# Cross-attention values as three products of rounded high and low parts, in a two-block transformer kernel

## The reference

```python
def memory_cross_attention(h, m, wq, wkv, wo):
    q = (h @ wq).reshape(B, S, XA_HEADS, XA_HEAD_DIM)      # 4 heads of 256
    kv = m @ wkv                                           # m: 256 normalised memory tokens
    k = kv[..., :D].reshape(B, -1, XA_HEADS, XA_HEAD_DIM)
    v = kv[..., D:].reshape(B, -1, XA_HEADS, XA_HEAD_DIM)
    s = jnp.einsum('bshd,bmhd->bhsm', q, k).astype(jnp.float32) * (XA_HEAD_DIM ** -0.5)
    p = jax.nn.softmax(s, axis=-1).astype(v.dtype)
    o = jnp.einsum('bhsm,bmhd->bshd', p, v).reshape(B, S, D)
    return o @ wo
```

## Time and profile before

| what | value |
|---|---|
| median of 3 runs | 986.03 us |
| the profiled execution, device time | 985.85 us |
| its span, first to last instruction | 984.0 us |
| PE busy (matmul) | 970.5 us, 99% |
| PE weight loads busy | 879.6 us, 89% |
| DVE busy | 685.7 us, 70% |
| ACT busy | 556.0 us, 57% |
| POOL busy | 207.1 us, 21% |
| granted TensorE clock, mean | 0.998 of 2.4 GHz |
| DMA | 172.94 MB, 176 GB/s |

### The profile page before, as it was taken

How to read it: one execution, slowest core, us unless ns; L and a number is a source line. 1 busy time by engine, 2 the same in 40 slices (tenths; PEclk the granted TensorE clock), 3 DMA queues, 4 the chain that set the end, 5 groups by cost and what they waited for, 6 DMA issues and landing times.

```text
span 984.0 us, 16670 instructions
## 1 busy us (share of the span) xinstructions
PE 970.5 (99%) x6532; PEld 879.6 (89%) x6532; DVE 685.7 (70%) x1057; ACT 556.0 (57%) x857; POOL 207.1 (21%) x197
## 2 busy tenths in 40 slices
PE   9999999999999999999999999999999999999997
PEld 7779769989988988898899899998898989989985
DVE  5789776854666587575566779776687666767973
ACT  5556674675765474555455466555445555546662
POOL 0002033300344540021003015121044301202610
PEclk9999999999999999999999999999999999999999
DMA  9644517465334447355414654467546433555431
GB/s 363 241 135 169 174 42 264 164 214 215 129 129 144 173 134 270 110 188 197 172 53 168 211 211 171 171 213 279 175 168 256 171 129 109 191 181 187 169 149 43
DMA packets 24832, 172.94 MB, mean 176 GB/s; under 512 B 2752, under 2 KB 2880, under 8 KB 4416
## 3 DMA queue, kind: packets, MB, share of 16 engines
q1 hardware_dynamic: 23040, 160.66, 46.0%
q10 hardware_dynamic: 1728, 11.40, 3.1%
HBM read 166.81 MB, written 5.24 MB: 175 GB/s over the span
## 4 chain that ended last, share of the span: by engine, by line
PE 95%; DVE 1%; ACT 1%; DMA 1%; POOL 1%; issue 0%; SPq 0%; ACTq 0%; DVEq 0%
PE banks L537 37%; PE banks L628 16%; PE banks L543 14%; PE banks L545 7%; PE banks L535 6%; PE banks L690 4%; PE banks L744 2%; DMA raw<-w 1%; PE banks L795 1%; PE banks L796 1%; PE banks L777 1%; PE banks L760 1%; PE banks L958 1%; PE banks L875 0%; PE banks L975 0%; PE banks L492 0%
## 5 line engine op out<-in xcount | busy, mean ns | idle before, releaser
L1648 DVE TENSOR_TENSOR wl<-raw,wh 128x1024 fp32r<-128x1024 f32 x300 | 379.0, 1273 | 151.5 <-ACT wh L1132 150.0
L1132 ACT ACTIVATE wh<-raw 128x1024 fp32r<-128x1024 f32 x300 | 313.4, 1054 | 175.6 <-PE banks L537 69.0
L543 PE MATMUL banks<-xx,wh 128*128 128x512 f32 x544 | 192.5, 398 | 0.0
L537 PE MATMUL banks<-xx,wh 128*128 128x256 f32 x1024 | 190.3, 285 | 0.0
L537 PE MATMUL banks<-yy,wh 128*128 128x256 f32 x1000 | 183.5, 285 | 0.1
L537 PEld LDWEIGHTS banks<-xx,wh 128*128 128x128 f32 x1024 | 161.5, 192 | 1.4 <-issue 0.5
L537 PEld LDWEIGHTS banks<-yy,wh 128*128 128x128 f32 x1000 | 156.9, 192 | 1.4 <-issue 0.8
L545 PE MATMUL banks<-xx,wl 128*128 128x256 f32 x544 | 151.9, 279 | 0.0
L537 PE MATMUL banks<-xx,wl 128*128 128x256 f32 x512 | 145.0, 283 | 0.0
L537 PE MATMUL banks<-yy,wl 128*128 128x256 f32 x500 | 136.8, 283 | 0.0
L543 PEld LDWEIGHTS banks<-xx,wh 128*128 128x128 f32 x544 | 102.1, 188 | 22.7
(11 more groups left out here) (227 smaller groups left out, 1462.3 us busy)
## 6 DMA issues: line engine op xcount, KB each, us to landing
raw<-w SPq DMA_DIRECT2D x149, 1024.0 KB, 4.8
m_scratch<-yy ACTq DMA_DIRECT2D x2, 1024.0 KB, 5.2
k_scratch<-kt ACTq DMA_DIRECT2D x2, 1024.0 KB, 7.0
kt<-k_scratch ACTq DMA_DIRECT2D x2, 1024.0 KB, 5.8
yy<-m_scratch ACTq DMA_DIRECT2D x2, 1024.0 KB, 6.8
raw<-w SPq DMA_DIRECT2D x2, 512.0 KB, 5.3
h<-xt SPq DMA_DIRECT2D x2, 512.0 KB, 6.1
v<-memt ACTq DMA_DIRECT2D x1, 1024.0 KB, 7.8
```

The source lines that it names most:

```text
L537: return pe.matmul(b[:, j, :], weights, o_[:, kk, :], start=k0 + k == 0 and q == 0 and (j == 0 or not both_open), stop=k0 + k == KT * p.de ...
L543: pe.matmul(b[:, j, :], wh[:, slot, j, k * P:k * P + P], operand[:, :, tile0 + k0 + k, :], start=k0 + k == 0, stop=False, skip_group_check ...
L1132: act.activation(wh[:, n % 2, j, :], raw[:, n % RAW_SLOTS, j, :], ACT.Copy).then_inc(hi_ready, 1)
L1648: dve.tensor_tensor(wl[:, n % 2, j, :], raw[:, n % RAW_SLOTS, j, :], wh[:, n % 2, j, :].bitcast(F32), ALU.subtract).then_inc(lo_ready, 1)
```

## The change

In X0 and X1 the values and the transposed probabilities are kept as fp32r high and low parts. PE multiplies high probabilities with high and with low values, and then low probabilities with high values. ACT's two evacuations now write the rounded part (`v_r`, and the first of `turned_parts`), and DVE gets two new kinds of instruction: `values_low` (4 per layer, in the value projection) and `turned_low` (4 per layer, in the attention). Both read the PSUM bank that ACT has just copied. The new tensors are other views of memory that is already there (`vl_r` lies in the upper half of `qz`). Two semaphores, `mv_low` and `p_low`, are new.

```diff
@@ project and project_tokens, PE
+                if p.name == "qx1":
+                    pe.wait_ge(mv_low, 8)
...
                                 pe.wait_ge(evac[p.prev.reader], p.prev.end)
+                                if name == "qx0":
+                                    pe.wait_ge(mv_low, 4)
...
                             if c >= 2 and c % 2 == 0 and half == 0:
                                 pe.wait_ge(evac[p.reader], p.base + c - 1 + t)
+                                if name[0:2] == "vx":
+                                    pe.wait_ge(mv_low, 4 * int(name[2]) + 1 + t)
@@ turn_probs, PE
                     pe.wait_ge(t_evac, u - 1)
+                    if name[0] == "X":
+                        pe.wait_ge(p_low, 4 * int(name[1]) + a - 1)
@@ values, PE
-                    for o, sl in value_ops(a):
-                        pe.matmul(o, v[:, 0, sl], wk(4 + a % 2)[:, 0:S], start=True, stop=False)
-                        mm = pe.matmul(o, v[:, 1, sl], wk(4 + a % 2)[:, S:2 * S], start=False, stop=True)
+                    if name[0] == "X":
+                        i = int(name[1])
+                        if a == 0:
+                            pe.wait_ge(mv_low, 4 * i + 4)
+                        for low in range(2):
+                            if low:
+                                pe.wait_ge(p_low, 4 * i + a + 1)
+                            pr = turned_parts(a)[low]
+                            for j, (o, sl) in enumerate(value_ops(a)):
+                                for q in range(2):
+                                    for part in (v_r, vl_r)[0:1 if low else 2]:
+                                        mm = pe.matmul(o, part[:, q, sl], pr[:, S * q:S * q + S],
...
@@ memory_values, ACT
-                act.activation(v[:, t, columns(c)], b, ACT.Copy, scale=rt_m[:, t:t + 1]).then_inc(act_evac, 1)
+                act.activation(v_r[:, t, columns(c)], b, ACT.Copy, scale=rt_m[:, t:t + 1]).then_inc(act_evac, 1)
@@ DVE
+            def values_low(l):
+                p = PH["vx" + l]
+                def f(c):
+                    if c % 2:
+                        for t in range(2):
+                            at = slice(CW * (c - 1), CW * (c + 1))
+                            dve.wait_ge(act_evac, p.base + c + t)
+                            dve.scalar_tensor_tensor(vl_r[:, t, at], bank[p.pair + t][:, :], rt_m[:, t:t + 1],
+                                                     v_r[:, t, at].bitcast(F32), ALU.mult, ALU.subtract).then_inc(mv_low, 1)
+            def turned_low(name, a):
+                if a >= 2:
+                    dve.wait_ge(o_full, OBASE[name] + a - 1)
+                dve.wait_ge(t_evac, UBASE[name] + a + 1)
+                high, low = turned_parts(a)
+                dve.tensor_tensor(low, bank[6 + a % 2][:, :], high.bitcast(F32), ALU.subtract).then_inc(p_low, 1)
@@ plain_low, DVE
                 def f(t):
+                    if name[0] == "X" and 2 <= t < 6:
+                        turned_low(name, t - 2)
...
-                    chunks("vx1", split=3)
+                    chunks("vx1", split=3, between=values_low("1"))
...
-                    chunks("vx0")
+                    chunks("vx0", between=values_low("0"))
```

More of the change, by code:

```diff
@@ L218, in build, with rounded_view @@
         yh, yl = [yy[:, q, :, :] for q in range(2)]
+        def rounded_view(name, shape):
+            with nc.sbuf_tensor(name, shape, F32R) as r:
+                return r
+        qz_r = rounded_view("qz_r", [P, NH, S])
         qz = sb("qz", [P, NH, S])
         kt = sb("kt", [P, KT, S])
+        v_r = rounded_view("v_r", [P, 2, D])
         v = sb("v", [P, 2, D])
         gt = sb("gt", [P, KT, S])
+        work_r = rounded_view("work_r", [P, 12 * 512])
         work = sb("work", [P, 12 * 512])
@@ L340, in turned, with turned_parts @@
             return wk(4 + a % 2)
+        vl_r = qz_r[:, 8:16, :].rearrange("p a b -> p (a b)").rearrange("p (t n) -> p t n", t=2)
+        def turned_parts(a):
+            return [work_r[:, 512 * i:512 * i + 512] for i in (4 + a % 2, 7 + a % 2)]
         def turned_kept(name):
@@ L405, in build @@
         m_hi, m_lo = sem("m_hi"), sem("m_lo")
+        mv_low, p_low = sem("mv_low"), sem("p_low")
         bias_ready, zero_ready, padded = sem("bias_ready"), sem("zero_ready"), sem("padded")
@@ L793, in values @@
                         pe.wait_ge(dve_evac, PH["fourier" if name == "N" else "q" + name.lower()].end)
-                    for o, sl in value_ops(a):
-                        pe.matmul(o, v[:, 0, sl], wk(4 + a % 2)[:, 0:S], start=True, stop=False)
-                        mm = pe.matmul(o, v[:, 1, sl], wk(4 + a % 2)[:, S:2 * S], start=False, stop=True)
+                    if name[0] == "X":
[10 more added lines that the diff above has]
+                                        mm = pe.matmul(o, part[:, q, sl], pr[:, S * q:S * q + S],
+                                                       start=j == q == low == 0 and part is v_r, stop=low == q == 1,
+                                                       skip_group_check=True)
+                    else:
+                        for o, sl in value_ops(a):
+                            pe.matmul(o, v[:, 0, sl], wk(4 + a % 2)[:, 0:S], start=True, stop=False)
+                            mm = pe.matmul(o, v[:, 1, sl], wk(4 + a % 2)[:, S:2 * S], start=False, stop=True)
                     mm.then_inc(o_full, 1)
@@ L1238, in turned_out @@
                 n = 3 * P if name == "A" else 4 * P
-                act.activation(turned(name, a)[:, 0:n], bank[6 + a % 2][:, 0:n], ACT.Copy).then_inc(t_evac, 1)
+                dst = turned_parts(a)[0] if name[0] == "X" else turned(name, a)
+                act.activation(dst[:, 0:n], bank[6 + a % 2][:, 0:n], ACT.Copy).then_inc(t_evac, 1)
             def soft_attention(name, heads, high, lag, start=1):
@@ L1818, in gated @@
                 return f
+            def values_low(l):
[7 more added lines that the diff above has]
+                                                     v_r[:, t, at].bitcast(F32), ALU.mult, ALU.subtract).then_inc(mv_low, 1)
+                return f
+            def turned_low(name, a):
[4 more added lines that the diff above has]
+                dve.tensor_tensor(low, bank[6 + a % 2][:, :], high.bitcast(F32), ALU.subtract).then_inc(p_low, 1)
             def plain_low(name, tiles, first):
```

## The result

The changed kernel takes **991.48 us** (median of 6 runs, 990.65 to 992.03), the kernel before 985.91 us beside it (6 runs, 985.68 to 986.04): ratio 1.0056, 95% interval 1.0046 to 1.0067. It is slower by 5.6 us, twice the 2.7 that were forecast, and it lies above the stated range. The profiled execution took 991.42 us, its span 989.6 us, at a mean granted clock of 0.995.

A forecast was written before the change was run, and what follows sets the result against it. PE was taken as the bound everywhere, busy 99% of the span. Terms of -2.3, 0, +0.6 and +4.4 us summed to +2.7 us on the median of 986.03, giving 988.7 us; the range over the cases was 987.3 to 990.7.

The forecast's parts named there:

- Term 1: Attentions X0 and X1: twelve fp32r matmuls replace four fp32 ones per head, 0.29 us gained for each of 8 heads, -2.3 us.
- Term 2: Attentions: four new turned_low DVE operations per layer, for which PE does not have to wait, 0 us.
- The rival in which DVE sets the pace: Attentions: DVE's extra 0.7 us per head gives back all the products' gain, 991.0 us; chance 0.08.
- Term 3: vx0, chunk 2: PE waits for the new values_low operation to read the first bank, +0.6 us.
- Term 4: vx1, chunk 2: PE waits for values_low, queued on DVE behind two weight splits, one stretched beside POOL, +4.4 us.
- The clock: vx1's wait: the summed forecast included no loss from a falling PE clock.
- The first rival: vx1's wait: the clock falls while PE is idle, costing 1.6 us more, 990.3 us; chance 0.18.
- The rival on the other side: vx1, chunk 2: DVE reaches the bank early, the wait is 0.8 us and the kernel not slower, 985.1 us; chance 0.08.

The follow-up runs named there:

- f2: The changed kernel with products back to four fp32 matmuls per head on the high parts, all new DVE work and waits kept: 993.23 us.
- e4: The changed kernel with chunks 2 and 3 of vx0 and vx1 writing to the other pair of PSUM banks: 983.66 us.
- f3: The kernel before, with its fp32 products, with chunks 2 and 3 of vx0 and vx1 in the other pair of banks: 985.57 us.
- g1: The changed kernel with the other pair of banks for chunks 2 and 3 in vx1 only, vx0 keeping its wait: 984.51 us.
- f1: The kernel before with PE's wait at chunk 2 of vx1 extended to DVE's second weight split, a gap of 3.9 us: 992.35 us.
- g2: The kernel before with PE's wait at chunk 2 of vx1 extended to DVE's third weight split, a gap of 6.12 us: 993.77 us.
- e2: The changed kernel with the first pair of values_low in vx1 put ahead of one weight split: 988.66 us.
- f0: The kernel before with PE's wait at chunk 2 of vx1 extended to DVE's first weight split, a gap of 1.72 us: 987.45 us.
- e3: The changed kernel with the first values_low pair in vx1 ahead of both weight splits, right behind the last convolution step: 986.05 us.

## Why the prediction was right and wrong

- **The direction** was right, and for the stated reason: the wait in vx1 is larger than what the products give.
- **Term 1, the products, -2.3 us.** The price per head was exact (1.43 to 1.44 us predicted and measured). The sum was mis-sized: -1.8 us by the starts of the records and by f2 against the changed kernel, -1.9 in e4 against f3. The piece that failed is "all of it is on the path": 0.27 us per layer comes back before ox, whose first matmul follows the last short product later than it followed the last fp32 one. No wait is listed for it but "issue"; f2 ties it to the short matmuls, and why it arises was not tested.
- **Term 2, `turned_low`, 0 us.** Right. No wait of PE for it is in the list of waits, and its eight instances take 683 to 692 ns, as the earlier trace rows. The rival in which DVE sets the pace did not occur; that its 991.0 us lies close to the measured time is chance, since nothing of its mechanism is in the profile.
- **Term 3, vx0, +0.6 us.** +0.76 by the starts of the records, 0.7 by g1 and e4. The new operation takes 736 to 751 ns and not 0.70: I took a two-operand operation's time for one with a per-partition scalar as well.
- **Term 4, vx1's wait, +4.4 us.** +4.45. The account of DVE's queue held piece by piece: the stretched split is 2.07 us and the operation that reads PSUM is not stretched, 0.74 us beside a busy POOL.
- **The clock** is the step that failed: the forecast put its loss in vx1's wait at nothing, and it was 2.3 us in the profiled execution. The first rival named it and its place. It got a chance of 0.18 because "PE would be idle only just over a microsecond longer" than the one instance, as if 3.3 us were the least gap that matters. f1, g2, f2, e2 and the changed kernel all lost the clock, the shortest gap being 2.4 us; 1.7 us (f0) and 1.25 us (e3) left it alone. With a gap forecast at 4.4 us this case should have carried most of the chance. Its price was a second error: 1.6 us, from the warm-up, is what the profiled executions of f1 and g2 lost, but that of the changed kernel lost 2.3. (5.26 less 3.5 is 1.8; the 1.6 comes out from start to start, 5.26 - 0.28 less 31 x 0.11.) Sum with that case: 986.03 + 2.7 + 2.3 = 991.0, and 0.5 for term 1 and 0.2 for term 3 make 991.7, beside 991.48 measured.
- **The rival on the other side**, DVE early, did not happen by itself, but e3 made it happen: with the pair right behind the convolution the time is within 0.2% of before. I had put its point at a gap of 3.7 us; e2 shows it lower, since at 2.4 us the clock takes 1.5 us more.

The Trainium skill (TensorE: Matmul & The Clock Gate, section on HAM oscillation) says that PE comes back cold from idle gaps and that one pays for it again each time. The runs agree in kind: 1.4 to 2.3 us lost for a gap of 2.4 to 6.1 us. The gap of 2.4 us in e2 is shorter than those that the section warns of, and here the measurement decides. The page's first part says of the rise at a kernel's start that its point varies from run to run. For the fall no two profiles of one kernel are at hand to show that: it came 2.0, 2.6, 2.7, 4.0 and 4.4 us after the last matmul in e2, g2, the changed kernel, f2 and f1, five kernels with one profile each.

What is open: why the changed kernel's work at 1.2 GHz lasted 4.9 us and that of the others 2.9 to 3.4, and whether any gap between 1.7 and 2.4 us is safe. The moments at which the clock changed are read from one profiled execution of each kernel; of the other runs there are the time and the mean granted clock alone. The four times of f1 hint that the length varies from execution to execution and does not belong to a kernel.

## What to carry to other kernels

Before a producer's bank or buffer gets a second reader, read what stands in front of that reader in its own queue; here two weight splits, not the new work, made 3.3 of the 4.4 us of wait (e3 against the changed kernel), and a bank that was free anyway made it zero. A new gap of 2.4 us or more in a dense TensorE stream cost 1.4 to 2.3 us on top of itself in each of the five profiled executions here, so price it with the clock. Where a faster product shortens PE's work, look at what follows the last of them: here the next matmul came later and took back 0.27 of 1.16 us per layer. And compare starts of records rather than positions in the chain where one side has a gap and the other has none.

## What was not expected of the hardware

- A gap of 2.4 us between dense matmuls brought the clock down to 1.2 GHz (e2, seven times within 988.56 to 988.83 us), one of 1.7 us did not (f0, ten runs within 987.26 to 987.73).
- The clock can fall after PE has resumed (f1, 0.5 us after), and its cost did not grow with the gap: 1.6 us at 3.9 and at 6.1 us in the profiled executions, with 1.1 us between the four times of the first (f1).
- A DVE operation that takes an operand from PSUM and one from SBUF keeps its time beside POOL (744 ns median, 751 at most), while the split ahead of it, both operands in SBUF, takes 2.07 us instead of 1.23.
